# First input projection of a two-block transformer kernel: rope's rotation moved from TensorE to GpSimd, and the gate product done in two passes instead of three

## What is computed

```
proj = h @ w_in                                   # h: 1024 tokens x 1024
qk_ml, v_ml, o_ml, gates, q_at, kv_at = split(proj)
i_pre = gates[..., :4] + ml_i_b                   # 4 heads
logf  = log_sigmoid(gates[..., 4:] + ml_f_b)
q_at  = rope(q_at.reshape(B, S, 8, 64), pos)      # 8 query heads of 64
k_at  = rope(kv_at[..., :128].reshape(B, S, 2, 64), pos)

def rope(x, pos):                                 # half = 32
    x1, x2 = x[..., :half], x[..., half:]
    return concatenate([x1 * cos - x2 * sin, x2 * cos + x1 * sin])
```

## Time and profile before

| what | value |
|---|---|
| time, median of 3 runs | 2306.46 us (2305.16 to 2307.43) |
| span of the profiled execution | 2307.9 us |
| PE busy | 2218.0 us, 96% of the span |
| DVE busy | 1617.7 us, 70% |
| ACT busy | 1089.5 us, 47% |
| POOL busy | 795.6 us, 34% |
| gate product on PE | 70.94 to 81.98 us |
| P2 to P6 with the five rotations | 81.98 to 145.25 us |
| gate rows turned, then P7 | 145.25 to 148.54, to 162.40 us |

### The profile page before, as it was taken

One profiled execution on the slowest core, in us unless ns is written; L12 is line 12 of the kernel. 1 busy time (PEld: TensorE's weight loads), 2 busy tenths in 40 slices (PEclk: granted clock), 3 DMA queues, 4 the chain that ended last, 5 costly groups with the idle time before them and its releaser, 6 DMA issues. The chain is left out here.

```text
span 2307.9 us, 29073 instructions
## 1 busy us (share of the span) xinstructions
PE 2218.0 (96%) x10136; PEld 1787.9 (77%) x10136; DVE 1617.7 (70%) x2247; ACT 1089.5 (47%) x1877; POOL 795.6 (34%) x579
## 2 busy tenths in 40 slices
PE   6999998999899999999998999999999999999998
PEld 4778887686678888888876767767778888887887
DVE  6468447626999999985797379994575555556686
ACT  5232256735644444455445368882343333334533
POOL 1030024513533232342023626661274444433310
PEclk9999999999999999999999999999999999999999
DMA  9156622033133333289944230003422333339986
GB/s 348 56 174 212 203 85 64 26 128 115 45 111 101 105 101 110 81 296 394 335 165 139 72 101 19 23 5 110 145 69 98 107 101 106 101 119 320 354 277 228
DMA packets 282565, 331.82 MB, mean 144 GB/s; under 512 B 18281, under 2 KB 180409, under 8 KB 282049
## 3 DMA queue, kind: packets, MB, share of 16 engines
q1 hardware_dynamic: 279760, 322.57, 41.4%
q0 software_dynamic: 2208, 7.37, 0.9%
q10 hardware_dynamic: 465, 0.17, 0.0%
HBM read 251.11 MB, written 78.94 MB: 143 GB/s over the span
## 5 line engine op out<-in xcount | busy, mean ns | idle before, releaser
L2643 PE MATMUL ps<-sum_hi,whi 128*128 128x512 f32 x640 | 249.5, 390 | 1.0 <-DVE wlo L2809 0.7
L2645 PE MATMUL ps<-sum_hi,wlo 128*128 128x512 f32 x640 | 249.0, 389 | 0.0
L2644 PE MATMUL ps<-sum_lo,whi 128*128 128x512 f32 x640 | 249.0, 389 | 0.0
L2669 PE MATMUL ps<-sum_lo,whi 128*128 128x512 f32 x616 | 240.7, 391 | 2.0 <-ACT arena L2754 2.0
L2671 PE MATMUL ps<-sum_lo,wlo 128*128 128x512 f32 x616 | 239.7, 389 | 0.0
L2670 PE MATMUL ps<-sum_lo,whi 128*128 128x512 f32 x616 | 239.7, 389 | 0.0
L2643 PE MATMUL ps<-hhi,whi 128*128 128x512 f32 x480 | 188.3, 392 | 9.0 <-DVE cbuf L3324 3.3
L226 DVE TENSOR_TENSOR wlo<-raw,whi 128x1024 fp32r<-128x1024 f32 x56 | 78.4, 1406 | 159.6 <-ACT whi L221 159.5
L2644 PE MATMUL ps<-hlo,whi 128*128 128x512 f32 x480 | 188.2, 392 | 0.0
L2645 PE MATMUL ps<-hhi,wlo 128*128 128x512 f32 x480 | 188.0, 392 | 0.0
L1732 POOL TENSOR_TENSOR cbuf<-cbuf,attn_stats 128x1024 f32<-128x1024 f32 x80 | 151.5, 1894 | 94.0 <-DVE attn_stats L1993 94.0
(11 more groups left out here) (450 smaller groups left out, 5575.2 us busy)
## 6 DMA issues: line engine op xcount, KB each, us to landing
shared<-ffn_blocks SPq DMA_DIRECT2D x154, 256.0 KB, 5.1
lead_work<-in_w_down SPq DMA_DIRECT2D x105, 256.0 KB, 4.4
arena<-in_w_down SPq DMA_DIRECT2D x100, 256.0 KB, 4.1
raw<-in_w_up SPq DMA_DIRECT2D x36, 512.0 KB, 5.1
ffn_blocks<-chunk_work SPq DMA_DIRECT2D x66, 256.0 KB, 2.3
ffn_blocks<-lead_work SPq DMA_DIRECT2D x66, 256.0 KB, 2.3
raw<-in_w_in SPq DMA_DIRECT2D x32, 512.0 KB, 4.7
arena<-in_w_ada SPq DMA_DIRECT2D x32, 512.0 KB, 5.5
```

Source lines behind the costliest of these rows:

```text
L2643: nc.tensor.matmul(o, hi[:, ws], mhi, start=fresh and k == 0, stop=False, skip_group_check=True)
L2644: nc.tensor.matmul(o, hi[:, ws], mlo, start=False, stop=False, skip_group_check=True)
L2645: mm = nc.tensor.matmul(o, lo[:, ws], mhi, start=False, stop=(k == 3), skip_group_check=True)
L2669: nc.tensor.matmul(o, hi[:, ws], mhi, start=fresh, stop=False, skip_group_check=True)
```

## The change

It has two parts.

1. **Rotation.** `rotA` and its five pairs of matmuls are gone from PE. POOL first negates two quarters of the sine table (32 rows each), then for each roped tile runs four products of 32 x 1024: a quarter of `cbuf` times the same quarter of the sines, written to the neighbouring quarter of `turned_sin`. DVE's `rope` keeps two instructions instead of three, waits for POOL's fourth product, and stands behind the gate steps of the same t instead of ahead of them. POOL's five rotations are put into its list between the spills and the query stores.
2. **Gates.** High and low weight columns lie side by side as one 128-column operand per slice, so that two passes (high activations, low activations) give all four partial products, the high ones in PSUM rows 0 to 63 and the low ones in 64 to 127. ACT copies four groups of rows instead of two, and DVE adds them with two more instructions of 4 x 1024.

The counts on the semaphores follow. One matrix less is set up at the start.

```diff
             for hf in range(2):
                 for k in range(DK):
-                    o = gates_out[0:64, tok]
-                    nc.tensor.matmul(o, gateR[:, 0, k, :], hhi[:, k, tok], start=(k == 0), stop=False)
-                    nc.tensor.matmul(o, gateR[:, 0, k, :], hlo[:, k, tok], start=False, stop=False)
-                    mm = nc.tensor.matmul(o, gateR[:, 1, k, :], hhi[:, k, tok], start=False, stop=(k == DK - 1))
+                    o, both = gates_out[:, tok], gate_w[:, k, :, :].rearrange("p i b -> p (i b)")
+                    nc.tensor.matmul(o, both, hhi[:, k, tok], start=(k == 0), stop=False)
+                    mm = nc.tensor.matmul(o, both, hlo[:, k, tok], start=False, stop=(k == DK - 1))
             mm.then_inc(gate_sum, 1)
-
-            def rotate(n):
-                t = ROPED[n]
-                pe.wait_ge(raw_copied, t + 1)
-                if n:
-                    pe.wait_ge(rope_step, 3 * n - 2)
-                for hf in range(2):
-                    tok = slice(hf * HALF, (hf + 1) * HALF)
-                    mm = nc.tensor.matmul(down[0][:, tok], rotA[:, :], cbuf[:, t % 4, tok], start=True, stop=True)
-                mm.then_inc(rotated, 1)
...
                 product(pe, up[t % 2], At(t))
-                if 2 <= t <= 6:
-                    rotate(t - 2)
...
+                    nc.scalar.activation(row_w, gates_out[64:68, :], ACT.Copy).then_inc(gate_row, 1)
+                    nc.scalar.activation(row_m, gates_out[96:100, :], ACT.Copy).then_inc(gate_row, 1)
...
-                dve.wait_ge(rotated, r + 1)
-                nc.vector.tensor_tensor(turned_sin, down[0][:, :], sin_1, ALU.mult).then_inc(rope_step, 1)
+                dve.wait_ge(rotated, 4 * r + 4)
                 nc.vector.tensor_tensor(c, c, cos_1, ALU.mult).then_inc(rope_step, 1)
-                dve.wait_ge(rope_step, 3 * r + 2)
+                dve.wait_ge(rope_step, 2 * r + 1)
                 nc.vector.tensor_tensor(c, c, turned_sin, ALU.add).then_inc(rope_step, 1)
...
-                dve.wait_ge(gate_row, 2)
+                dve.wait_ge(gate_row, 4)
+                link(nc.vector.tensor_tensor(row_i, row_i, row_w, ALU.add))
+                link(nc.vector.tensor_tensor(row_z, row_z, row_m, ALU.add))
...
-                if 2 <= t <= 6:
-                    rope(t - 2)
                 if t == 2:
                     gates_first()
                 if t == 3:
                     gates_scans()
                 if t == 4:
                     gates_exponents()
+                if 2 <= t <= 6:
+                    rope(t - 2)
...
         def in_pool(pool):
+            pool.wait_ge(sines_in, 16)
+            for quarter in (32, 96):
+                rows_ = slice(quarter, quarter + 32)
+                nc.gpsimd.tensor_scalar(sin_1[rows_, :], sin_1[rows_, :], -1.0, 0.0, ALU.mult, ALU.add).then_inc(sines_turned, 1)
+            pool.wait_ge(sines_turned, 2)
+
+            def rotate(r):
+
+                t = ROPED[r]
+                pool.wait_ge(raw_copied, t + 1)
+                if r:
+                    pool.wait_ge(rope_step, 2 * r)
+                for quarter in (0, 32, 64, 96):
+                    src, dst = slice(quarter, quarter + 32), slice(quarter ^ 32, (quarter ^ 32) + 32)
+                    nc.gpsimd.tensor_tensor(turned_sin[dst, :], cbuf[src, t % 4, :], sin_1[src, :], ALU.mult)\
+                      .then_inc(rotated, 1)
+                pool.wait_ge(rotated, 4 * r + 4)
+
+            rotate(0)
...
+            rotate(1)
+            rotate(2)
             query(0)
-            pool.wait_ge(g_dve, 8)
+            pool.wait_ge(g_dve, 10)
             pool.dma_start(rows_dram, row_a).then_inc(rows_stored, 16)
+            rotate(3)
             query(1)
+            rotate(4)
             query(2)
```

More of the change, by code:

```diff
@@ L145, in block_kernel @@
         pairF = sb("pairF", [P, P])
-        rotA = sb("rotA", [P, P])
         rotB = sb("rotB", [P, P])
@@ L520, in _ @@
                 ch = Chain(pool, s_pool, pool_n)
-                for m in (par_in, identF, onesF, pairF, rotA, rotB, causal, selF, band):
+                for m in (par_in, identF, onesF, pairF, rotB, causal, selF, band):
                     ch.step(nc.gpsimd.memset(m[tuple([slice(None)] * len(m.shape))], 1.0 if m is onesF else 0.0))
@@ L536, in _ @@
                     ch.link(nc.gpsimd.memset(pairF[64 * b:64 * b + 64, 64 * b:64 * b + 64], 1.0))
-                for m, h in ((rotA, 32), (rotB, 16)):
+                for m, h in ((rotB, 16),):
                     v = m[:, :].rearrange("k (g s j) -> k g s j", s=2, j=h)
@@ L582, in _ @@
                 pe.sem_inc(used, RING)
-                pe.wait_ge(s_pool, 11)
+                pe.wait_ge(s_pool, 10)
                 pe.wait_ge(s_c, 16)
@@ L911, in block_kernel @@
         spilled = [sem(f"spilled{i}") for i in range(4)]
+        sines_in, sines_turned = sem("rope1_sines"), sem("rope1_sines_turned")
         tables_in, raw_copied, rotated, rope_step = (sem("rope1_" + x) for x in ("tables", "copied", "rotated", "steps"))
@@ L924, in block_kernel @@
         gates_out = down[1]
+        gate_w = gateR[:, :, :, :].rearrange("p i a b -> p (i a b)").rearrange("p (k i b) -> p k i b", i=2, b=64)
         ROPED = (0, 2, 3, 4, 5)
@@ L966, in in_sp @@
             sp.dma_start(cos_1, a["rope"][:, 0, :]).then_inc(tables_in, 16)
-            sp.dma_start(sin_1, a["rope"][:, 1, :]).then_inc(tables_in, 16)
+            sp.dma_start(sin_1, a["rope"][:, 1, :]).then_inc(sines_in, 16)
             for t in range(4, N_IN + 4):
@@ L971, in in_sp @@
                     if n == 0:
-                        sp.wait_ge(rope_step, 3 * len(ROPED))
+                        sp.wait_ge(rope_step, 2 * len(ROPED))
                     if n == 3:
@@ L1039, in in_act @@
             act.wait_ge(gate_loaded, 32)
-            nc.scalar.activation(gateR[:, 0, :, :], gateF[:, :, :], ACT.Copy).then_inc(gate_hi, 1)
+            nc.scalar.activation(gate_w[:, :, 0, :], gateF[:, :, :], ACT.Copy).then_inc(gate_hi, 1)
             for t in range(2):
@@ L1047, in in_act @@
                     n = t - 4
-                    act.wait_ge(rope_step, 3 * n + 6)
+                    act.wait_ge(rope_step, 2 * n + 4)
                     if n >= 2:
@@ L1055, in in_act @@
                         nc.scalar.preload_act_table_set(LN_EXP)
-                        act.wait_ge(g_dve, 13)
+                        act.wait_ge(g_dve, 15)
                     for c in range(4 * (t - EXP_FROM - 1), 4 * (t - EXP_FROM)):
@@ L1093, in in_act @@
                       .then_inc(gate_row, 1)
+                    nc.scalar.activation(row_w, gates_out[64:68, :], ACT.Copy).then_inc(gate_row, 1)
+                    nc.scalar.activation(row_m, gates_out[96:100, :], ACT.Copy).then_inc(gate_row, 1)
                 if t == 2:
-                    act.wait_ge(g_dve, 4)
+                    act.wait_ge(g_dve, 6)
                     nc.scalar.activation(row_a, row_a, ACT.Exp, scale=-1.0).then_inc(g_act, 1)
@@ L1099, in in_act @@
                 if t == 5:
-                    act.wait_ge(g_dve, 12)
+                    act.wait_ge(g_dve, 14)
                     nc.scalar.activation(row_w, row_w, ACT.Exp).then_inc(g_act, 1)
@@ L1116, in rope @@
                 if r == 0:
-                    dve.wait_ge(tables_in, 32)
-                else:
-                    dve.wait_ge(rope_step, 3 * r)
-                dve.wait_ge(rotated, r + 1)
-                nc.vector.tensor_tensor(turned_sin, down[0][:, :], sin_1, ALU.mult).then_inc(rope_step, 1)
+                    dve.wait_ge(tables_in, 16)
+                dve.wait_ge(rotated, 4 * r + 4)
                 nc.vector.tensor_tensor(c, c, cos_1, ALU.mult).then_inc(rope_step, 1)
-                dve.wait_ge(rope_step, 3 * r + 2)
+                dve.wait_ge(rope_step, 2 * r + 1)
                 nc.vector.tensor_tensor(c, c, turned_sin, ALU.add).then_inc(rope_step, 1)
@@ L1154, in in_dve @@
             dve.wait_ge(gate_hi, 1)
-            nc.vector.tensor_tensor(gateR[:, 1, :, :], gateF[:, :, :], gateR[:, 0, :, :].bitcast(F32),
+            nc.vector.tensor_tensor(gate_w[:, :, 1, :], gateF[:, :, :], gate_w[:, :, 0, :].bitcast(F32),
                                     ALU.subtract).then_inc(gate_hi, 1)
@@ L1204, in in_pool @@
         def in_pool(pool):
+            pool.wait_ge(sines_in, 16)
[14 more added lines that the diff above has]
+            rotate(0)
             for t in range(2):
                 if t == 0:
-                    pool.wait_ge(rope_step, 3)
+                    pool.wait_ge(rope_step, 2)
                 else:
@@ L1327, in gains_of @@
                                         ALU.mult).then_inc(c_gain, 1)
-            pool.wait_ge(g_dve, 13)
+            pool.wait_ge(g_dve, 15)
             multiplied(pool, At(N_IN - 1))
@@ L1437, in chunk_pe @@
             pe.wait_ge(late_done, 6 - ADA_FIRST)
-            pe.wait_ge(g_dve, 13)
+            pe.wait_ge(g_dve, 15)
             turn(0)
```

## The result

The changed kernel takes **2314.81 us** (median of 19 runs, 2310.97 to 2321.6); the kernel before, on the same chip, 2306.59 us (19 runs). The ratio is 1.0036, with a 95% interval of 1.0028 to 1.0045: 6.5 to 10.4 us slower. The forecast was 2315.0. The profiled execution has a span of 2313.0 us, against 2307.9.

What follows compares the result with a forecast made beforehand. PE, busy 96% of the span, was taken to bound the kernel; despite 12.5 us less work, P8 starts 5.5 us later and loses 3.0 to clock: 8.5 on the median 2306.46 gives 2315.0 us, range 2293 to 2321.

Steps and rivals of the forecast that it cites:

- What PE loses: Gate product sheds sixteen matmuls, 3.7 us; five rotations leave PE, 8.8 us; together 12.5 us less PE work.
- The price of a product: Each 32 x 1024 POOL product of a rotation: 2.4 us alone, 2.2 in a turn; bounds 0.6 and 2.9.
- first rival: POOL's four quarter products run side by side, a rotation takes about 3 us, program 2294.0 us; chance 0.22.
- dearer 2.9: Rival: POOL products cost 2.9 us, moving partitions a fifth more; sixteen add 8 to 9 us, 2324; chance 0.08.
- Turns: POOL products and DVE steps with two SBUF inputs do not overlap; a POOL product then costs 2.2 us.
- The prediction's sentence on two SBUF inputs: Every DVE step of gates, rope and low parts has two SBUF inputs; the convolution, reading PSUM, is left out.
- The chain: Gate steps, ropes, rotations and tile 6's convolution end at 167.8, so P8 starts at 167.9, 5.5 us later.
- The clock of P8: After PE stands still 13 us, P8 starts at half clock and takes 3.0 us longer.
- The sum: P8 is 5.5 us late plus 3.0 us of clock, 8.5 us behind, none of it gained back.
- No gain from the gates: Rival remark: the gates' 3.7 us are eaten by 2.2 of copies and 2.4 of adds; no separate chance.

Runs made afterwards that it cites:

- one product: Changed kernel with one 128 x 1024 POOL product per rotation instead of four of 32 x 1024, leaving out the quarter exchange: 2294.97 us, ratio 0.9944.
- DMA: Changed kernel with quarters exchanged by four SBUF-to-SBUF DMAs on ACT's queue into two buffers, DVE multiplying by the sines: 2293.84 us, ratio 0.9949.
- the run with unshifted quarters: Changed kernel with each quarter's product written to its own partitions, leaving out the exchange: 2312.76 us, ratio 1.0027.
- second trace: Changed kernel itself, unedited, run again on one chip beside later experiments: 2313.74 us, ratio 1.0031.
- the kernel with the gate part alone: Kernel before with only the two-pass gate product, four row copies and two adds; rotation stays on PE: 2300.38 us, ratio 0.998.
- the kernel with the fifty matmuls: Changed kernel with 50 needless 512-column matmuls between P7 and P8: 2315.89 us (1.0041), second time 2313.43 us (1.003).

## Why the prediction was right

The direction, the mechanism and the place were as forecast; the total is within 0.2 us, which is closer than the terms are.

* **What PE loses.** Gate product forecast 7.4, measured 7.25. P7 was to start at 140.9, and started at 140.18. With POOL's price removed (one product, DMA) the stage gave 14.1 and 14.2 us, for the 12.5 forecast. The rest may be clock: in the earlier trace rows P7 began at half clock, in those runs the loss there was smaller (0.98 against 0.96 over 70 to 163 us).
* **The price of a product.** Taken as 2.4 alone and 2.2 in a turn; measured 2.42 and 2.2. That excludes the quarter price of the first rival (0.6) and the dearer 2.9 for shifted partitions; the run with unshifted quarters shows that the shift is free.
* **Turns.** Forecast from one scan and a 4 x 7 copy; measured on most steps that met a rotation (3.3 to 4.4 us; one step under rotation 2 kept its 1.21). Rotations 1 and 2 were to end at 109.8 and 126.1, and ended at 109.1 and 125.3. The Trainium skill, SBUF — State Buffer, section "Who interferes with whom", says that a DVE instruction with two SBUF inputs contends with a GpSimd instruction that reads SBUF, and calls the shared ports an exclusive lock; the trace agrees (4.36 for 2.28), with 32 partitions on POOL's side and four on DVE's. The prediction's sentence on two SBUF inputs is too narrow: the 4 x 7 copy reads one operand, and it took 2.25 us under rotation 2 and 0.20 in the run with DMAs.
* **The chain.** The term that was mis-sized, by 2 us. Rotation 3 was to end at 143.1, rotation 4 at 159.2, the convolution at 167.8; they ended at 141.6, 157.5 and 165.8. The 2 us are spread over the chain: 0.8 was there at the end of rotation 2, another 0.8 came with the stores and gaps around query 0 (rotation 3 was put at 133.5 and began at 131.91), and the rest behind it. Counted from the gate product, P8 came 3.5 us later than before, and 3.6 in the second trace, instead of 5.5.
* **The clock of P8.** 3.0 forecast, 2.9 measured in the first trace of the change and 2.4 in the second; filling the wait gave 2.1 to 2.6 of it back in the stage. In the time of the whole program that gain was not seen.
* **The sum.** 3.5 + 2.9 = 6.4 in the stage, against 8.5. The program's 8.2 (6.5 to 10.4), and 4.6 to 9.9 in the second set, thus holds a microsecond or two that these two traces do not show. One place for it is the trace of the kernel before: its P7 lost 13.86 - 10.88 = 3.0 us to half clock, while the kernel with the gate part alone lost none behind the same small matmuls. In an execution of the kernel before without that loss P8 would start at 159.4, and the change would cost 9.4 in the stage (an estimate from these figures). The profiled execution of the kernel before was also a long one: the times of its other runs lie 1.8 us above their spans, which puts it at some 2309.7 (an estimate), 3.1 above the median. How often P7 begins at half clock is not known from one trace, so this is not shown. That the total came out at the forecast is partly chance.
* **No gain from the gates** was in the chain as a rival's remark, and holds only behind the rotation: alone they gave 5.7 us (3.7 of matmuls; the rest may be clock), together with it some 1.1 us of P8's start and nothing that the time shows.

## What to carry to other kernels

Price a GpSimd operation by its instructions and columns: cutting one over partitions into four quarters cost four times as much here, and each one can also hold up a DVE step that reads SBUF. When work is taken off the busiest engine, follow the other engine's chain to the next buffer that the busiest one needs; here 12.5 us came off TensorE and P8 still started 3.5 us later. Moving rows between partitions can be a DMA's work: twenty small transfers, landing in 2.4 us (median), replaced 20 x 2.42 = 48 us of products.

## What was not expected of the hardware

* Four 32 x 1024 products on four different quarters ran one behind the other, 9.77 us, with or without a move to other partitions; one of 128 x 1024 took 2.40.
* The two negations of 32 x 1024 on POOL (58.85, 3.96 us), which the prediction put down as nothing, stretched the last two norm steps on DVE. It stayed hidden: the gate product began at 70.90, as before. DVE's timeline of the kernel before and of the changed one:

```profile
60.02 2.59 DVE L508 SCALAR_TENSOR_TENSOR hlo<-cbuf,mod,hhi 128x1024 fp32r<-128x1024 f32 x2
```

```profile
59.83 4.04 DVE L507 SCALAR_TENSOR_TENSOR hlo<-cbuf,mod,hhi 128x1024 fp32r<-128x1024 f32 x2
```

* The granted clock falls at different places in executions of one kernel. From 365 to 375 us and from 375 to 385 us it was 1.00 and 0.68 in the first trace of the kernel with the fifty matmuls, 0.83 and 1.00 in the second. Longer runs go with a lower mean: of the 59 runs of the kernel before that were taken beside the experiments, the nine with a mean granted clock of 0.988 took 2309.6 us on average, the seven with 0.992 took 2302.6. A stage's time from a trace told apart 2 us that 5 to 12 runs of the whole did not, but it carries the clock of its own execution too, as P7 of the kernel before shows.
